# The short convolution's three input products of a two-block model on Trainium2: high and low input columns side by side in one wide product

## The reference, cut to what matters

```
proj = jnp.einsum('bld,de->ble', n, w_in[l])
z, xbc, dt_f, dt_b, sc_b, sc_c, sc_v = jnp.split(proj, SPLIT_POINTS, axis=-1)
...
def short_conv_branch(sc_b, sc_c, sc_v, conv_w):
    return sc_b * dwconv_centred(sc_c * sc_v, conv_w)     # 3 taps over the tokens
...
yg = yg * lax.rsqrt(jnp.mean(yg * yg, axis=-1, keepdims=True) + RMS_EPS)   # state-space branch, by group
```

## Time and profile before

| | |
|---|---|
| median of 3 runs | 1712.71 us (1712.66 to 1712.94) |
| the profiled execution's own time | 1712.69 us |
| its span in the trace | 1710.9 us |
| PE busy | 1687.9 us (99%) |
| PEld busy | 1518.0 us (89%) |
| DVE busy | 1329.8 us (78%) |
| ACT busy | 960.1 us (56%) |
| chain of work that ended last | PE 87%, DVE 11% |

### The profile page before, as it was taken

One profiled execution on the slowest core, in us unless ns is written; L12 is line 12 of the kernel. 1 busy time (PEld: TensorE's weight loads), 2 busy tenths in 40 slices (PEclk: granted clock), 3 DMA queues, 4 the chain that ended last, 5 costly groups with the idle time before them and its releaser, 6 DMA issues.

```text
span 1710.9 us, 28028 instructions
## 1 busy us (share of the span) xinstructions
PE 1687.9 (99%) x11216; PEld 1518.0 (89%) x11216; DVE 1329.8 (78%) x2074; ACT 960.1 (56%) x1584; POOL 60.9 (4%) x81
## 2 busy tenths in 40 slices
PE   8999999999999999999999999999999999999998
PEld 7999888888999988888899999888889999978886
DVE  6867678888877758878899888766678988786666
ACT  5567556565656646665645754544454476454443
POOL 2000000000200000000000001000000000100001
PEclk9999999999999999999999999999999999999999
DMA  7544555555555446555566455555546644455652
GB/s 224 177 145 136 172 172 185 186 196 160 177 151 155 145 159 200 197 189 188 165 200 194 149 173 174 183 188 187 192 153 216 197 149 170 139 197 197 197 189 82
DMA packets 233007, 299.73 MB, mean 175 GB/s; under 512 B 6163, under 2 KB 198317, under 8 KB 232877
## 3 DMA queue, kind: packets, MB, share of 16 engines
q1 hardware_dynamic: 232569, 297.82, 53.6%
q10 hardware_dynamic: 308, 0.12, 0.0%
HBM read 292.67 MB, written 1.05 MB: 172 GB/s over the span
## 4 chain that ended last, share of the span: by engine, by line
PE 87%; DVE 11%; issue 1%; ACT 1%; POOL 0%; DVEq 0%; ACTq 0%; POOLq 0%
PE ring_banks L516 64%; PE bank L516 16%; DVE weights_lo L1605 4%; PE bank L807 1%; DVE conv_sums L2011 1%; PE bank L918 1%; PE bank L929 1%; PE ring_banks L712 1%; PE bank L755 0%; PE bank L792 0%; DVE norm_statistics L1712 0%; PE bank L953 0%; PE bank L815 0%; POOL norm_small L1070 0%; PE bank L718 0%
## 5 line engine op out<-in xcount | busy, mean ns | idle before, releaser
L1605 DVE TENSOR_TENSOR weights_lo<-raw_weights,weights_hi 128x1024 fp32r<-128x1024 f32 (+1 forms) x552 | 645.8, 1210 | 110.2 <-ACT weights_hi L1172 108.9
L516 PE MATMUL ring_banks<-input_parts,weights_hi 128*128 128x256 f32 (+1 forms) x4384 | 695.5, 312 | 6.5 <-issue 2.4
L516 PEld LDWEIGHTS ring_banks<-input_parts,weights_hi 128*128 128x128 f32 x4384 | 615.7, 191 | 54.8 <-issue 9.5
L1172 ACT ACTIVATE weights_hi<-raw_weights 128x1024 fp32r<-128x1024 f32 (+1 forms) x552 | 544.2, 1036 | 193.2 <-PE ring_banks L516 97.5
L516 PE MATMUL ring_banks<-input_parts,weights_lo 128*128 128x256 f32 x2752 | 373.9, 283 | 0.0
L516 PEld LDWEIGHTS ring_banks<-input_parts,weights_lo 128*128 128x128 f32 x2752 | 355.2, 192 | 5.5
L516 PE MATMUL bank<-weights_hi,hidden_hi 128*128 128x512 f32 x432 | 110.7, 392 | 0.0
L516 PE MATMUL bank<-weights_lo,hidden_hi 128*128 128x512 f32 x432 | 109.3, 389 | 0.0
L516 PE MATMUL bank<-weights_hi,hidden_lo 128*128 128x512 f32 x432 | 109.3, 389 | 0.0
L2011 DVE SCALAR_TENSOR_TENSOR conv_sums<-conv_padded,params_second_layer,conv_sums 128x256 f32<-128x256 f32 x240 | 98.8, 478 | 0.0
L516 PEld LDWEIGHTS bank<-weights_lo,hidden_hi 128*128 128x128 f32 x432 | 81.1, 188 | 16.9
(11 more groups left out here) (262 smaller groups left out, 1735.1 us busy)
## 6 DMA issues: line engine op xcount, KB each, us to landing
raw_weights<-in_w_in SPq DMA_DIRECT2D x104, 1024.0 KB, 5.3
raw_weights<-in_w_ff SPq DMA_DIRECT2D x64, 1024.0 KB, 5.2
raw_weights<-in_w_ffn_up SPq DMA_DIRECT2D x44, 1024.0 KB, 5.0
raw_weights<-in_w_ffn_down SPq DMA_DIRECT2D x22, 1024.0 KB, 4.8
raw_weights<-in_w_out SPq DMA_DIRECT2D x16, 1024.0 KB, 5.1
raw_weights<-in_w_o SPq DMA_DIRECT2D x8, 1024.0 KB, 5.1
pair<-pair SPq DMA_DIRECT2D x64, 64.0 KB, 2.8
raw_weights<-in_w_diff_out SPq DMA_DIRECT2D x4, 1024.0 KB, 5.1
```

The source lines that it names most:

```text
L516: return mm(o, w, x, start=first, stop=last, skip_group_check=True)
L1172: A(whi[:, t, i * n:(i + 1) * n], raw[:, s, i * n:(i + 1) * n], ACT.Copy).then_inc(hi_done, 1)
L1605: tt(wlo[:, t, r], raw[:, s, r], whi[:, t, r].bitcast(f32), SUB).then_inc(w_ready, 1)
```

## The change

The 12 chunks of the short convolution (13 to 24) in both layers are computed by `gemm_wide` in place of `gemm`. ACT copies the low-input half of each of the three chunks to SBUF (`wide_low`, two banks at once), where before it copied one chunk of three. DVE adds the other half to it, `parts_added`, three times a group. The two multiplications of DVE then read only SBUF. The banks are given back by the additions, and the counts on which PE waits are changed to the two-bank pattern. The core of the diff:

```diff
@@ PE
+                    elif c < 13:
+                        gemm(c, cx, u, ux, [ring[u % RING]], 8, 256, nh, nl)
+                        u += 1
                     else:
-                        gemm(c, cx, u, ux, [ring[u % RING]], 8, 256, nh, nl)
+                        gemm_wide(c, cx, ux + u + (2 if c == 13 else 3), u)
                         u += 1
...
-                    pe.wait_ge(ring_free, ux + u + 2 * half + 2)
+                    pe.wait_ge(ring_free, ux + u + half + 3)
@@ ACT
                     multiplied(c, cx)
-                    A(tmp[0][:], pair(ring[u % RING]), ACT.Copy).then_inc(sc_mid, 1)
+                    A(tmp[0][:], wide_low(u), ACT.Copy).then_inc(sc_low, 1)
                     late(c)
                     split_hi(c + 2, cx, cr)
                     extras(c)
+                    multiplied(c + 1, cx)
+                    A(tmp[1][:], wide_low(u + 1), ACT.Copy).then_inc(sc_low, 1)
                     late(c + 1)
                     split_hi(c + 3, cx, cr)
-                    act.wait_ge(ring_free, ux + (u + RING + 2))
+                    act.wait_ge(sc_prod, l * 4 + j + 1)
                     for m in range(2):
                         k = 2 * j + m
                         last = A(tmp[2][:, m, :], tmp[1][:, m, :], ACT.Copy, scale=p1("sc_w", 8 + k))
                     last.then_inc(sc_mid, 1)
                     extras(c + 1)
+                    if j:
+                        act.wait_ge(mixsc_ready, l * 4 + j)
+                    multiplied(c + 2, cx)
+                    A(tmp[3][:], wide_low(u + 2), ACT.Copy).then_inc(sc_low, 1)
                     late(c + 2)
@@ DVE
-                    dve.wait_ge(sc_mid, l * 8 + 2 * j + 1)
-                    dve.sem_inc(ring_free, 1)
+
+                    def parts_added(i, x):
+                        dve.wait_ge(sc_low, l * 12 + 3 * j + i + 1)
+                        tt(x[:], wide_high(u + i), x[:], ADD).then_inc(ring_free, 1)
+
                     late(c)
                     split_lo(c + 2, cx)
+                    parts_added(0, tmp[0])
                     extras(c)
-                    multiplied(c + 1, cx)
-                    tt(tmp[1][:], tmp[0][:], pair(ring[(u + 1) % RING]), MUL).then_inc(ring_free, 1)
                     late(c + 1)
+                    parts_added(1, tmp[1])
+                    dve.wait_ge(ring_free, ux + (u + RING + 2))
+                    tt(tmp[1][:], tmp[0][:], tmp[1][:], MUL).then_inc(sc_prod, 1)
                     split_lo(c + 3, cx)
-                    dve.wait_ge(sc_mid, l * 8 + 2 * j + 2)
+                    dve.wait_ge(sc_mid, l * 4 + j + 1)
                     outer_taps(lambda m: tmp[2][:, m, :], lambda m: tmp[1][:, m, :], lambda tap, m: p1("sc_w", 8 * tap + 2 * j + m), None)
                     extras(c + 1)
-                    multiplied(c + 2, cx)
+                    late(c + 2)
+                    parts_added(2, tmp[3])
                     chain.sync()
-                    if j:
-                        dve.wait_ge(mixsc_ready, l * 4 + j)
-                    tt(tmp[3][:], tmp[2][:], pair(ring[(u + 2) % RING]), MUL).then_inc(pb_ready, 1)
+                    dve.wait_ge(ring_free, ux + (u + RING + 3))
+                    tt(tmp[3][:], tmp[2][:], tmp[3][:], MUL).then_inc(pb_ready, 1)
                     dve.wait_ge(pb_ready, l * 4 + j + 1)
-                    dve.sem_inc(ring_free, 1)
-                    late(c + 2)
                     split_lo(c + 4, cx)
```

More of the change, by code:

```diff
@@ L309, in build @@
         xbc_ready = sem("xbc_ready")
+        sc_low, sc_prod = sem("sc_low"), sem("sc_product")
         sc_mid, pb_ready, mixsc_hi, mixsc_ready = sem("sc_mid"), sem("pb_ready"), sem("mixsc_hi"), sem("mixsc_ready")
```

## The result

| | before | after |
|---|---|---|
| median | 1712.68 us (1712.39 to 1712.94, 4 runs) | 1726.04 us (1724.56 to 1726.34, 4 runs) |
| ratio | 1 | 1.0077, 95% interval 1.0065 to 1.0089 |
| span of the profiled execution | 1710.9 us | 1724.4 us |
| mean granted clock of PE | 0.999 | 0.994 |

The account below looks back on a forecast made before the run. PE was taken to set the pace, with little slack at the norms. Per layer, 6.9 us of waits less 12 x 0.19 = 2.3 gave 4.6 us, 9.2 in both: 1721.9 us, range 1717.5 to 1725.

Parts of the forecast that it names:

- PE's clock falls: Rival, chance 0.03: behind the 3.0 us wait the clock halves for one wide chunk a layer, 5.57 us each; 1733 us.
- the stop (3.0 us): At the norm behind chunk 19, PE waits 3.0 us for squares that end at 150.8.
- PE's gain: High weights' products in 24 chunks: 16 wide ones replace 32 narrow ones, gaining 4.6 us.
- The 0.19 of a chunk: High products of one chunk take 3.65 us wide against 3.84 narrow, a gain of 0.19 us.
- The waits: PE waits behind chunks 15, 19, 23 and 24: 1.1 + 3.0 + 2.1 + 0.7 = 6.9 us a layer.
- the addition followed by its multiplication: On DVE, an addition whose result the next operation needs holds the engine 0.87 us; bounds 0.60 and 0.90.
- The gap of 0.21: On DVE, the gap read behind L1883 when the next operation waits for a result of 0.69 us.
- the lateness when `split_lo(19)` starts: In DVE's queue ahead of the norm behind chunk 19: `split_lo(19)`, which started at 137.12, comes 2.7 us late.
- Behind chunk 24: PE reaches 189.2 and the diagonals are done at 189.9: a wait of 0.7 us.
- The price of the operations: On DVE, a 128x512 float32 operation takes 0.69 us with one operand in PSUM, 0.685 with both in SBUF.
- weight transfer was late: Rival, chance 0.02: one of SP's weight loads in each group comes 0.5 us late; 4 us more, 1726.
- the waits eat the gain: Rival, no change, chance 0.06: waits of 1.6 to 3.9 us a layer, time 1709.3 to 1716.1 us.

Follow-up runs that it names:

- kernel with filled stops: Changed kernel plus products of zeros on PE ahead of the norm, 10 behind chunk 19 and 6 behind 23: 1718.99 us, ratio 1.0036.
- run with both queues ordered: Changed kernel, gate and squares moved forward, ACT's second exponential ahead of the copies, DVE's root and diagonals ahead of low weights behind 19 and 23: 1710.50 us.
- run with the gates forward: Changed kernel with the state-space gate and its squares moved forward on DVE and ACT, past low weights or the third addition: 1714.19 us, ratio 1.0008.

## Why the prediction was wrong

**The failing step.** It is the rival "PE's clock falls", with a chance of 0.03 and nothing in the forecast's sum. The prediction had the stop (3.0 us) and the price of a fall, wrote that the stop is longer than any that PE has in this stage, and then took the clock of 1.00 in the earlier trace rows to hold. But those rows show a PE without a stop; they say nothing for the case that was forecast. The trace before has stops elsewhere, of 1.39 and 1.36 us and one of 2.01 at the program's start, and the clock stays at 1.00 behind all three, so it could not have shown the fall either. Filling the stops gave back 7.05 us, so the fall is a cost of its own; without it the kernel has 1718.99 us, inside the range. As the rival had it, one wide chunk would pay 5.57 us in each layer, 11.1 in all; it was 8.0 by the timeline, because the clock came back within the chunk, but behind two stops a layer and not one. That is more than the 7.05, in part because at full clock PE waits 0.3 us more a layer, at the spreading behind chunk 24. The Trainium skill (TensorE: Matmul & The Clock Gate, section HAM oscillation) describes waits of about 3 to 5 us between bursts that bring the clock to half; here it went to 0.50 behind stops of 1.25 and 2.2 us, which are shorter.

**PE's gain.** Predicted 4.6 us, 4.1 measured in the high parts. The 0.19 of a chunk holds where a chunk stands directly behind a chunk (3.65 against 3.84) or behind the spreading (3.72 against 3.91), five times a layer. Behind the other slots it is 3.75 to 3.78 against 3.91 to 3.94, some 0.16, seven times. The earlier trace rows had only the first case. (The expectation of the run with both queues ordered took it too low, at 1.9 us a layer.)

**The waits.** 9.1 us against 13.8. The places and the order were right: behind 15, 19 and 23, longest behind 19, with DVE's queue as the reason. Each was oversized: 0.79 for 1.1, 2.37 for 3.0, 1.41 for 2.1. The term was the addition followed by its multiplication, taken at 0.87. The rows of after give 0.72 and 0.79 from start to start:

```profile
138.36 0.68 DVE L1880 TENSOR_TENSOR pair<-ring_banks,pair 128x512 f32<-128x512 f32 x1
139.08 0.69 DVE L1889 TENSOR_TENSOR pair<-pair 128x512 f32<-128x512 f32 x1
...
143.66 0.68 DVE L1880 TENSOR_TENSOR pair<-ring_banks,pair 128x512 f32<-128x512 f32 x1
144.45 0.69 DVE L1898 TENSOR_TENSOR pair<-pair 128x512 f32<-128x512 f32 x1
```

The gap of 0.21 in the earlier trace rows is behind a different pair of operations. Behind chunk 19 the squares come 0.65 us earlier than forecast (all times less the 0.18 us by which chunk 13 starts later in this trace). Of this the lateness when `split_lo(19)` starts gives 0.3 (2.4 us for 2.7, half of it from ACT's second exponential and half from the addition), the second addition 0.26 (it lengthens its stretch by 0.61 for 0.87), and the stretch from the multiplication to the squares 0.1. Behind chunk 24, 0.7 was predicted and none came. In the kernel with filled stops, at full clock, 0.25 came; so most of it was oversized, and the rest was covered by PE's delay from the lower clock.

**The other steps.** The price of the operations held: the addition with one operand in PSUM has 0.68, the multiplication in SBUF 0.69. No chunk waited for a bank in the changed kernel, no weight transfer was late, and nothing was given back behind chunk 25. The forecast's sum, without the clock, was +9.2. With what was measured it is 9.1 of waits, 0.6 for norms that run 0.1 us longer behind each stop, less 4.3 of gain: +5.4, and with the clock's 8.0 it is the measured 13.4. (The kernel with filled stops has the +5.4 and 0.6 of waits at the spreading, near its measured +6.2.) The errors of size, together -3.8, hid nearly half of the missing 8.0 us, so it is luck that the forecast missed its range by 1 us only. One sum among the rivals is wrong: waits of 1.6 us a layer would give 1711.3 us; for the 1709.3 of "the waits eat the gain" they would have to be 0.6.

**What stays open.** What besides the length of the stop decides whether the clock falls. Ahead of the norm, stops of up to 0.64 us were followed by no fall, stops of 0.92 us by one in both layers, 1.02 and 1.74 in one of two layers, 1.25, 1.86, 2.2 and 3.2 in both. Elsewhere stops of such lengths had none: 0.83 to 0.96 us ahead of the spreading (the run with the gates forward, four stops), and two stops of 1.4 us in later stages, which all ten kernels have, the one before too:

```profile
1499.99 0.51 PE L516 MATMUL ring_banks<-weights_hi,hidden_hi 128*128 128x512 f32 x1 [1.36 <-DVE pair L2193]
```

The clock stayed at 1.00 behind these twenty. Behind them come products of 512 columns at once; behind a stop at the norm come its eight products of one column, 0.9 us of them. A stop of 2.0 us at the program's start was followed by a fall in two of the ten traces. Whether the products around the stop, its place in the program or chance decide was not tested.

## What to carry to other kernels

Where the engine that sets the pace has no slack, a forecast wait has to be priced twice, as the wait and as what the clock may lose behind it; here 9.1 us of waits brought 8.0 us more, all of it at the four stops of 1.25 us and over. An addition that is small against an engine's free share can still be the whole cost, so first look at how early the operation behind it in the queue is needed, and put what the pace-setting engine reads next ahead of it, on every engine of that chain. If a short stop can't be avoided, products of zeros can keep the clock up: here they gave back 7.05 us of 13.4.

## What was not expected of the hardware

- The fall does not come with the stop. The traces of five kernels show twelve falls in this stage. Eleven began 0.4 to 2.4 us after PE worked again, with the clock at 1.00 while it stood, and one began in the stop (3.20 us long), 1.0 us before its end. The clock was then at 0.50 for 3.4 us (nine falls) or 6.8 us (three), and nothing between was seen. A fall of 3.4 us costs 1.5 to 1.6 us, one of 6.8 costs 2.6 to 3.2.
- It isn't the same from one layer to the next: after stops of 1.74 and 1.75 us the clock fell once and held once, in one execution. And it isn't the length alone: stops of 1.4 us with wide products right behind them never brought it down, in twenty cases.
- A float32 operation of 128x512 on DVE that needs the result of the last one starts 0.72 to 0.79 us after it, and 0.60 if it doesn't (134.78 to 135.38 in the earlier trace rows). The Trainium skill (VectorE: DVE Perf Modes, section The DRAIN you can't avoid) says of eight copies that a semaphore after each costs nothing extra. It doesn't say whether they read one another; here the wait for the last result costs 0.1 to 0.2 us each time.
